# A deep single-core fp32 model kernel: the first unit's order, the order of products at stage boundaries, and a shorter path for HGRN2

## What is computed

```python
def first_block(x, ...):                       # DEPTH = 2
    for i in range(DEPTH):
        x = x + 0.5 * swiglu(rms_norm(x, ffn1_norm[i]), ffn1_w_gate[i], ffn1_w_up[i], ffn1_w_down[i])
        h = rms_norm(x, mix_norm[i])
        x = x + (moba_mixer(h, ...) if i % 2 == 0 else mamba2_mixer(h, ...))
        x = x + 0.5 * swiglu(rms_norm(x, ffn2_norm[i]), ffn2_w_gate[i], ffn2_w_up[i], ffn2_w_down[i])
    return x
...
def step(S, inp):                              # HGRN2, chunks of 64 tokens, 8 heads of 128
    qc, kc, lfc, vc = inp
    b = jnp.cumsum(lfc, axis=2)
    inter = jnp.einsum('bhtd,bhde->bhte', qc * jnp.exp(b), S)
    ...
    intra = jnp.einsum('bhts,bhse->bhte', A, vc)
    S_new = jnp.exp(b_last[:, :, 0, :])[..., None] * S + jnp.einsum(
        'bhsd,bhse->bhde', kc * jnp.exp(b_last - b), vc)
    return S_new, inter + intra
```

## Time and profile before

| | us |
|---|---|
| median of 3 runs | 1348.39 (1347.85 to 1348.75) |
| the profiled execution, its own time | 1349.01 |
| its span in the trace | 1347.2 |
| PE busy in the span | 1333.1 |
| DVE busy | 957.4 |
| ACT busy | 753.2 |
| POOL busy | 218.9 |

### The profile page before, as it was taken

How to read it: one execution, slowest core, us unless ns; L and a number is a source line. 1 busy time by engine, 2 the same in 40 slices (tenths; PEclk the granted TensorE clock), 3 DMA queues, 4 the chain that set the end, 5 groups by cost and what they waited for, 6 DMA issues and landing times.

```text
span 1347.2 us, 21455 instructions
## 1 busy us (share of the span) xinstructions
PE 1333.1 (99%) x8527; PEld 1157.2 (86%) x8527; DVE 957.4 (71%) x1026; ACT 753.2 (56%) x882; POOL 218.9 (16%) x199
## 2 busy tenths in 40 slices
PE   9999999999999999999999999999999999999997
PEld 7888888888888888888899988888888899888886
DVE  6666668857666676666677999667888766877586
ACT  6444455656444454444566678854444455657453
POOL 3500001101000020000000126220000001655740
PEclk9999999999999999999999999999999999999999
DMA  8665646526555555555544565488886554645341
GB/s 277 208 190 188 193 157 210 188 91 191 187 187 187 187 187 190 187 187 187 188 157 159 188 207 172 142 279 290 283 290 234 187 157 157 219 159 182 113 157 50
DMA packets 158292, 254.19 MB, mean 189 GB/s; under 512 B 8784, under 2 KB 99232, under 8 KB 156560
## 3 DMA queue, kind: packets, MB, share of 16 engines
q1 hardware_dynamic: 155136, 232.94, 53.4%
q0 software_dynamic: 2576, 18.45, 3.6%
q10 hardware_dynamic: 512, 1.85, 0.4%
HBM read 252.12 MB, written 1.08 MB: 188 GB/s over the span
## 4 chain that ended last, share of the span: by engine, by line
PE 97%; DVE 2%; ACT 1%; issue 0%; POOL 0%; POOLq 0%; DVEq 0%; ACTq 0%
PE psum L630 24%; PE psum L618 12%; PE psum L662 5%; PE psum L663 5%; PE psum L664 5%; PE psum L1910 4%; PE psum L1911 4%; PE psum L1912 4%; PE psum L450 3%; PE psum L451 3%; PE psum L452 3%; PE psum L429 3%; PE psum L431 3%; PE psum L430 3%; PE psum L1435 1%; PE psum L1436 1%
## 5 line engine op out<-in xcount | busy, mean ns | idle before, releaser
L391 DVE TENSOR_TENSOR w_lo<-raw,w_hi 128x2048 fp32r<-128x2048 f32 x220 | 512.7, 2332 | 204.8 <-ACT w_hi L383 204.5
L383 ACT ACTIVATE w_hi<-raw 128x2048 fp32r<-128x2048 f32 x220 | 420.6, 1912 | 174.6 <-PE psum L664 79.6
L630 PE MATMUL psum<-hT,w_hi 128*128 128x512 f32 x1408 | 335.8, 390 | 0.9 <-DVE hT L501 0.8
L630 PEld LDWEIGHTS psum<-hT,w_hi 128*128 128x128 f32 x1408 | 260.8, 188 | 54.2 <-issue 1.6
L618 PEld LDWEIGHTS psum<-hT,w_lo 128*128 128x128 f32 x1408 | 180.2, 191 | 6.5
L618 PE MATMUL psum<-hT,w_lo 128*128 128x256 f32 x1408 | 183.0, 283 | 0.0
L662 PE MATMUL psum<-w_hi,hidT_hi 128*128 128x512 f32 x320 | 125.0, 391 | 0.0
L663 PE MATMUL psum<-w_lo,hidT_hi 128*128 128x512 f32 x320 | 125.0, 391 | 0.0
L664 PE MATMUL psum<-w_hi,hidT_lo 128*128 128x512 f32 x320 | 124.5, 389 | 0.0
L507 POOL TENSOR_SCALAR meansq<-sumsq 128x2 f32<-128x2 f32 x7 | 6.0, 856 | 661.7 <-ACT xn L475 661.7
L712 ACT ACTIVATE hid<-psum 128x512 f32<-128x512 f32 x44 | 26.3, 598 | 150.7 <-PE psum L618 150.7
(11 more groups left out here) (381 smaller groups left out, 2049.9 us busy)
## 6 DMA issues: line engine op xcount, KB each, us to landing
raw<-in_ffn_w_up SPq DMA_DIRECT2D x88, 512.0 KB, 4.8
raw<-in_ffn_w_down SPq DMA_DIRECT2D x88, 512.0 KB, 4.2
raw<-in_ffn_w_gate SPq DMA_DIRECT2D x86, 512.0 KB, 4.7
raw<-in_w_in SPq DMA_DIRECT2D x72, 512.0 KB, 4.6
raw<-in_ssm_w_in SPq DMA_DIRECT2D x48, 512.0 KB, 4.6
raw<-in_attn_w_qkv SPq DMA_DIRECT2D x24, 512.0 KB, 4.7
ada_in<-in_w_ada POOLq DMA_DIRECT2D x8, 1536.0 KB, 8.2
raw<-in_ssm_w_out SPq DMA_DIRECT2D x16, 512.0 KB, 4.4
```

The costliest lines, as they stand in the source:

```text
L383: act.activation(w_hi[:, slot, :], raw[:, slot, :], ACT.Copy).then_inc(sem("hi_ready"), 1)
L391: dve.tensor_tensor(w_lo[:, slot, :], raw[:, slot, :], w_hi[:, slot, :].bitcast(F32), ALU.subtract)\
L630: pe.matmul(both, hi[:, k, at_:at_ + P], hT[:, k, :, :], start=k == 0, stop=False, skip_group_check=True)
```

## The change

**Start.** x comes as column halves: the first half (k 0 to 3) before gate's first two transfers, the second half (`x_late`) between gate's second and third. ACT asks for the norm's row before the constants. `keep_busy` is 7 and 3 instead of 10 and 4. PE turns k 0 to 3, makes the products of k 0 and 1, turns k 4 and 5, makes k 2, turns k 6 and 7, and goes on. The high parts of quarters 2 and 3 are made by POOL. DVE makes `hT_lo` 2 to 7 before the low quarters 1 to 3.

**Boundaries.** k 0 and k 1 have a PSUM bank each (`last_of_bank`), so `hT_hi` 0 waits for two turns instead of four. `linear_unit` and `turned_chunk` make, for all four k, the products with the high part of the activations first, on a wait for `hT_hi`, and then the four with the low part, on a wait for `hT`. The last unit of wo and of the ssm's projection is made token tile by token tile, and `add_half` adds token tile 0 while PE is in tile 1. (The second block's last unit already was in that form.)

**ssm.** In ACT's order `copy_z(0)` stands ahead of the last pair of convolution tiles, `group_squares(0)` moves from the end of step 4 to step 5, `group_squares(1)` from the start of step 7 to the end of step 6; POOL's `group_rstd(0)` moves from step 9 to 10.

**HGRN2.** No state is made. Tick JOIN makes the scores between different chunks directly: 16 products (chunk 2t by chunk 2t+1, 64 columns) and 32 (chunks 2 and 3 by chunks 0 and 1), all on column halves of PE. DVE prepares for them with two products, 128 x 512 each (`hg_far`), ACT copies the two results (`hg_next`, `hg_across`). OUT_A is 16 `both_chunks` (64 rows by 128 columns) in turn with 16 `second_chunk` (64 by 64), and 8 products `hg_across` by `hg_v` on the whole array. Gone are K_ROWS, STATES_12, STATE_3, the copies by ACT and the 16 updates by DVE.

```diff
-BUSY_BEFORE_X, BUSY_AFTER_X = 10, 4
+BUSY_BEFORE_X, BUSY_AFTER_X = 7, 3
...
 def linear_unit(pe, unit, k0, tiles, a_hi, a_lo, banks, ready=None):
...
                 if ready:
+                    pe.wait_ge(sem(ready[0] + "_hi"), ready[1] + k + 1)
+                for t in range(TT):
+                    a = a_hi[:, k, t * P:(t + 1) * P]
+                    pe.matmul(psum[:, banks[t], :], a, hi[:, kk, :], start=k == 0, stop=False)
+                    pe.matmul(psum[:, banks[t], :], a, lo[:, kk, :], start=False, stop=False)
+            for kk in range(4):
+                k = k0 + kk
+                if ready:
                     pe.wait_ge(sem(ready[0]), ready[1] + k + 1)
                 for t in range(TT):
-                    to = psum[:, banks[t], :]
+                    m = pe.matmul(psum[:, banks[t], :], a_lo[:, k, t * P:(t + 1) * P], hi[:, kk, :], start=False,
+                                  stop=k == tiles - 1)
...
+        def last_of_bank(k):
+
+            return k if k < 2 else k | 1
...
             for k in ks:
-                act.wait_ge(sem("xT"), KD * n + (k | 1) + 1)
+                act.wait_ge(sem("xT"), KD * n + last_of_bank(k) + 1)
...
+                    if k == 4:
+                        load_half_of_x(sp, 1, "x_late")
...
+            pool.wait_ge(sem("landed_0"), 16 * PARTS)
+            for k in (2, 3):
+                cs = first_part(k)
+                pool.tensor_copy(w_hi[:, 0, cs], raw[:, 0, cs]).then_inc(sem("late_hi"), 1)
...
+        def turn_late_x(pe, k):
+
+            if k == 2:
+                pe.wait_ge(sem("x_late"), 16 * TT)
+            if k in (2, 3):
+                turn_x(pe, 0, x, (2 * k, 2 * k + 1))
...
             hT_lo_tiles(dve, 0, ("ffn1_norm", 0), (0, 1))
             first_lo(0)
+            hT_lo_tiles(dve, 0, ("ffn1_norm", 0), (2, 3, 4, 5, 6, 7))
             first_lo(1)
-            hT_lo_tiles(dve, 0, ("ffn1_norm", 0), (2, 3))
             first_lo(2)
-            hT_lo_tiles(dve, 0, ("ffn1_norm", 0), (4, 5))
-            first_lo(3)
-            hT_lo_tiles(dve, 0, ("ffn1_norm", 0), (6, 7))
+            first_lo(3).then_inc(sem("lo_ready"), 1)
...
+            for t in range(TT):
+                for k in (6, 7):
+                    wo_tile(3, k, (t,))
...
+            if i == JOIN:
                 pe.wait_ge(sem("hg_decayed"), 2)
                 pe.wait_ge(sem("hg_att"), STEPS)
+                chunk = lambda c: slice(c * HG_C, (c + 1) * HG_C)
+
                 for n in range(HEADS * TT):
                     h, t = divmod(n, TT)
-                    m = pe.transpose(psum[:, 4 + n // 4, n % 4 * P:(n % 4 + 1) * P],
-                                     hg_k[:, h, t * P:(t + 1) * P], ident)
-                    if n % 8 == 7:
-                        m.then_inc(sem("hg_k_turned"), 1)
...
+                    m = pe.matmul(psum[0:HG_C, 4 + n // 8, n % 8 * HG_C:(n % 8 + 1) * HG_C],
+                                  hg_k[:, h, chunk(2 * t)], hg_q[:, h, chunk(2 * t + 1)], start=True, stop=True)
+                m.then_inc(sem("hg_joined"), 1)
+
+                pe.wait_ge(sem("hg_far"), 2)
                 for h in range(HEADS):
...
+                    for c, q in ((2, hg_q), (3, hg_pair)):
+                        for rows, k in ((0, hg_pair), (1, hg_k)):
+                            at_ = h % 4 * P + (c - 2) * HG_C
+                            m = pe.matmul(psum[chunk(rows), 6 + h // 4, at_:at_ + HG_C],
+                                          k[:, h, chunk(rows)], q[:, h, chunk(c)], start=True, stop=True)
+                m.then_inc(sem("hg_joined"), 1)
             if i == OUT_A:
...
+                for t in range(TT):
+                    for n, h in enumerate((0, 4, 1, 5, 2, 6, 3, 7)):
+                        both_chunks(h, t)
+                        if n:
+                            second_chunk((0, 4, 1, 5, 2, 6, 3, 7)[n - 1], t)
+                    m = second_chunk(7, t)
+                    for h in range(HEADS if t else 0):
+                        m = pe.matmul(psum[:, 6 + h // 4, h % 4 * P:(h % 4 + 1) * P], hg_across[:, h, :],
+                                      hg_v[:, 0, h * P:(h + 1) * P], start=False, stop=True, skip_group_check=True)
+                    m.then_inc(sem("out_a_ready"), 1)
```

More of the change, by code:

```diff
@@ L441, in turned_chunk @@
                 hi, lo = use_unit(pe, unit + j)
+                tiles = [(c, psum[:, banks[c // 2], (c % 2) * SEQ:(c % 2 + 1) * SEQ], slice(c * P, (c + 1) * P))
+                         for c in range(4)]
+                for kk in range(4):
+                    k = 4 * j + kk
+                    if ready:
+                        pe.wait_ge(sem(ready[0] + "_hi"), ready[1] + k + 1)
+                    for c, to, cs in tiles:
+                        pe.matmul(to, hi[:, kk, cs], hT_hi[:, k, :], start=k == 0 and c % 2 == 0, stop=False,
+                                  skip_group_check=True)
+                        pe.matmul(to, lo[:, kk, cs], hT_hi[:, k, :], start=False, stop=False, skip_group_check=True)
                 for kk in range(4):
@@ L445, in turned_chunk @@
                         pe.wait_ge(sem(ready[0]), ready[1] + k + 1)
-                    for c in range(4):
-                        to = psum[:, banks[c // 2], (c % 2) * SEQ:(c % 2 + 1) * SEQ]
-                        a, b = hi[:, kk, c * P:(c + 1) * P], lo[:, kk, c * P:(c + 1) * P]
-                        pe.matmul(to, a, hT_hi[:, k, :], start=k == 0 and c % 2 == 0, stop=False, skip_group_check=True)
-                        pe.matmul(to, a, hT_lo[:, k, :], start=False, stop=False, skip_group_check=True)
-                        m = pe.matmul(to, b, hT_hi[:, k, :], start=False, stop=k == KD - 1, skip_group_check=True)
+                    for c, to, cs in tiles:
+                        m = pe.matmul(to, hi[:, kk, cs], hT_lo[:, k, :], start=False, stop=k == KD - 1,
+                                      skip_group_check=True)
                 m.then_inc(sem("unit_used"), 1)
@@ L1863, in build @@
         STEPS = 2 * (LEVELS + 1)
-        K_ROWS, STATES_12, STATE_3, OUT_A, RET_TURN, RET_SCORES, RET_STATE, OUT_B = range(STEPS + 3, STEPS + 11)
+        JOIN, OUT_A = STEPS + 3, STEPS + 4
+        RET_TURN, RET_SCORES, RET_STATE, OUT_B = range(STEPS + 7, STEPS + 11)
         def second_sp(sp):
```

236 lines of the change are left out of this document (111 added, 125 removed).

## The result

The changed kernel takes 1357.34 us (median of 6 runs, 1356.76 to 1357.98) against 1348.30 us of the kernel before beside it: a ratio of 1.0066, 95% interval 1.0054 to 1.0078. The forecast was 1341.3 us, with a range up to 1348.6. It is slower by 9 us, and the range did not hold it. The profiled execution took 1357.49 us, its span 1355.7.

A forecast was written before the change was run, and what follows sets the result against it. PE bounds the kernel, with 97% of the chain. Gains of 3.8 (HGRN2), 2.6 (boundaries), 0.5 (ssm) and 0.2 (start) sum to 7.1 us: 1349.0 becomes 1341.9, median 1341.3 us; range 1339.6 to 1348.6.

The forecast's parts named there:

- OUT_A's products overlap: OUT_A in HGRN2: 64 passes on different row halves overlap at 0.058 us each, 3.7 us; OUT_A 5.5 us in all.
- The first rival: OUT_A: each change of shape drains PE, 0.32 us a product, OUT_A 12 us, total 1347.8 us; chance 0.28.
- My own point of no gain: OUT_A: at 0.34 us a product the whole change makes nothing; slower by over 0.2% from 0.42.
- HGRN2 missed its forecast: Second block: four interruptions of 13.6 us become 9.7, gain 3.9 us, 3.8 after 0.1 for DVE and POOL.
- The second rival: OUT_A: each of 64 passes waits its whole latency, 0.27 us; OUT_A 19.1 us, total 1354.9 us; chance 0.07.
- JOIN: HGRN2's direct scores between chunks: 3.7 us, with PE not waiting for DVE's `hg_far`.
- The boundaries: Norms 1 to 6: shorter gaps between turns and products, 2.6 us gain, bounds 1.3 and 3.2.
- The ssm: PE's two stops for banks freed by z's copy: 0.5 us gain, between 0 and 1.5; early arrival mostly waits at scores.
- The first stop: ssm: PE's 1.04 us wait at 792.52 for banks freed by z's copy; said to go.
- The start: Unit 0's low weights start at 14.6 instead of 14.78, a 0.2 us gain; bounds -1.0 and +0.8.
- The lower bound: Start: -1.0 us, from late x or POOL casts, or fewer `keep_busy` delaying the clock's rise.

The follow-up runs named there:

- one-shape kernel: Changed kernel with second chunk's products zero-padded to 64 rows by 128 columns, token tiles crossed over between PSUM banks; 1342.69 us, again 1343.39 us.
- runs of two: Changed kernel with OUT_A's products in runs of two of one shape, 16 changes of shape instead of 32; 1353.86 us.
- kernel with pairs in three gaps: Changed kernel with OUT_A's alternating products spread over three gaps between chunks (5, 5 and 6 pairs); 1352.98 us.
- grouped: Changed kernel with OUT_A's products grouped by tile shape, eight of each per token tile, four changes of shape instead of 32; 1346.10 us.

## Why the prediction was wrong

**OUT_A's products overlap: wrong, and it decides everything.** The step that failed is "If pairs overlap in the same way, 64 x 0.058 is 3.7 us", worked out from products that alternate between two row halves in one shape. Here the shape changed at every product, and OUT_A took 20.3 us instead of 5.5. The rate was right (0.055, in the one-shape kernel), but it belongs to one shape. Nearly the whole difference between forecast and result is this step: the one-shape kernel, which only restores its condition, came in at 1342.7 and 1343.4.

**The first rival had the mechanism, and a price too low.** It put 0.32 us on a product; the trace has 0.387 (five pairs in 3.87 us, 1244.37 to 1248.24). At that price alone OUT_A would be 32 x 0.387 + 1.8 = 14.2 us. My own point of no gain was 0.34 us a product, so the drains alone put the change at 7.1 - 8.7 = -1.6 us, at about 1350. The Trainium skill, "TensorEngine Tiling (Array Packing)", section "Key Properties", says that a change of mode drains the engine. The traces agree: 0.39 us a product with a change, 0.24 without. It was given 0.28, which was too little: no row stood behind a free change between the two shapes. But its evidence was weaker than the prediction has it. Not each change in the trace of before shows 0.17 to 0.35 us of idle weight loads. Going into small products it is mostly 0.35 in the second block and mostly 0.04 to 0.13 in the ssm; coming out of them it is 0.04 to 0.20 where PE did not wait (0.04 at 1158.78, 0.07 at 800.41), and between two ordinary loads of a chunk it is 0.04.

**What no rival had: the clock.** I asked of the clock only at the start. From 1248.26 to 1265.33 PE was granted 0.50, and that cost 20.3 - 14.2 = 6.1 us in OUT_A and 0.9 in the chunk behind (four products in 1.79 us instead of 0.91). Drains 8.7 and clock 7.0 make 15.7 us; HGRN2 missed its forecast by 11.7 + 3.8 = 15.5 in the traces and by 10.8 + 3.8 = 14.6 by the runs. The second rival's 1354.9 came near the result with another mechanism, the whole latency for each pass (0.27), which the first 5 us refute (0.19).

**JOIN: right.** 3.9 us against 3.7, and PE did not wait for `hg_far`. DVE's two products took 1.1 and 1.2 us beside POOL instead of 0.7, and this time lay under the first 16 products.

**The boundaries: right, a little too small.** 2.6 forecast, 3.1 in the trace (0.4 at norms 1 and 3, 0.6 at 2 and 5, 0.5 at 4, 0.7 at 6), inside the stated bounds, and 3.9 by the runs, whose interval holds both.

**The ssm: right that the stop moves on, size open.** The first stop went or shrank to 0.5 us at most, and 0.4 to 0.9 us of waiting for `cross` came in nine of eleven profiles. 0.5 was forecast; one pair of kernels says 0.75, the other 0.7 or nothing, the traces nothing that stands out of their scatter.

**The start: wrong in sign.** 0.2 gain forecast, a loss of 0.65 to 1.7 us in the pairs that differ in the start alone, and of 0.8 on the mean in the profiles' turns of norm 1. The low weights were forecast at 14.6 and came at 14.25, but they were not the term. I had worked out no time for the first whole unit, though the diff puts two more issues ahead of it on SP. They moved it from 3.83 to 4.60, and ACT waited 1.75 us for it. In the profiles this landing sets the time of everything behind it. The lower bound that I had named, a late rise of the clock, was seen in one profile (10.86).

Step by step from before, by medians: the boundaries -3.9 (1344.60), start and ssm together +2.0 (1346.59), HGRN2 +10.8 (1357.34). The middle step is the least certain: on the one-shape HGRN2 the same two parts cost 0.25 or 0.95 us (1342.44 to 1342.69 or 1343.39).

## What to carry to other kernels

Treat a change of PE's tile shape as a price of about 0.15 to 0.3 us each (0.39 us a product with a change, against 0.24 on one row half and 0.11 where row halves overlap), and count the changes before counting the columns saved. (The prices are those of products with 64 rows and 128 columns.) Group products by shape, or pad one kind with zeros to the other's shape, so that row halves can overlap. Where a stretch of small products with changes of shape lasts some microseconds, look at the granted clock of the whole neighbourhood: the profile calls PE busy in it, and the big products behind pay too. When a transfer is put ahead of others at the start, work out when each of the others will be issued, and who waits for it.

## What the runs showed of the hardware

A PE that is 100% busy in the profile can lose its clock. In the changed kernel it was busy for 3.00 us of each 3, while its weight loads were for 1.8 to 2.1 only; the time lost between products shows in that, in their starts and in the granted clock. Before the clock fell (at 1248.26), PE had run six pairs of small products with a change of shape at each product, 4.9 us, or in the runs of two four groups of four with two changes each, 4.9 us too. In the kernel with pairs in three gaps it fell in the last products of the second part, 3.1 us after the part's start, although an ordinary chunk lay between the parts. Before it rose, PE had run three products of 512 columns and was in the fourth (the changed kernel), or six (three gaps). In the grouped and the one-shape kernels it did not fall. Its price, 7.0 us, was nearly that of the drains, 8.7.
